# Decoder layer on one core: new homes for five tensors that hold ring places, x in quarters, last pair without a dispatch

## The chip, the cores and the metric

The kernel runs on one core of one Trainium2 chip (trn2), written in Bass with explicit semaphores: every engine (TensorE, VectorE, ScalarE, GpSimd, SyncE) has its own instruction stream, and SyncE and GpSimd also issue the transfers. The metric is the time of one execution on the device in microseconds (us).

## The reference

One layer over 256 tokens of width 1024, all in float32. The mixer normalises x, projects it with `w_in`, and runs three branches: causal differential attention (8 heads, two softmax maps each), a pooling mixer, and cross-attention into 256 memory tokens. Each branch has a gate; the merged result goes through `w_out` and is added to x. Then a mixture of 32 experts, 4 for each token:

```python
proj = rmsnorm(h, g_mix) @ w_in
q, k, v, u_pool, q_mem, gate_logits = split(proj)
g = sigmoid(gate_logits + b_gates)                 # three gates
h = h + (g[0]*y_attn + g[1]*y_pool + g[2]*y_mem) @ w_out
logits = rmsnorm(h, g_ffn) @ w_router + b_router   # top 4 of 32
g = minimum(xb @ w_gate[e] + b_gate[e], 7); u = clip(xb @ w_up[e] + b_up[e], -7, 7)
out = g * sigmoid(1.702 * g) * (u + 1) @ w_down[e] + b_down[e]
```

Each expert has three matrices of 1024 x 1024, 4.19 MB each: 402.65 MB in all, read once.

## The kernel before

**Mixer.** The weights come as 22 pieces (`PIECES`, L54) of two halves of 1 MB each, which SyncE loads in that order into five buffers `raw0` to `raw4`, in turn (`load`, L451; a half waits in `half_free`, L400, for the half five before it). A piece gives two units of 128 tokens (`UNITS`, L68). For the first piece TensorE multiplies in float32 (L1476). For all others ScalarE makes a rounded copy of the half (`hi`, L693), VectorE the remainder (`lo_whole`, L973), and TensorE three products for each block (L1483). The stationary operand is split in the same way: x into `XNT`, the memory into `MEMT`, the attention output into `OT`, the merged result into `MGT`. A unit writes one of three banks in turn and waits until the unit three before it has been read out of that bank (`bank_read`). Units 36 to 39 are branch a's gates (pieces ga0, ga1, halves 32 to 35), units 40 to 43 the attention map (wba0, wba1, halves 36 to 39), 44 to 47 `w_out`. `add_bias` (L1166) adds a gate's bias, which GpSimd has fetched into the gate's place (`gate_bias`, L615), and `gate_exp` (L704) applies the tanh. `merge` (L1185) multiplies with the branch. Head h of the attention takes the turn of the weights (`turn_a`), two units, the turn of the previous head's output and the values product. The order is written out by hand on every engine.

**Ring.** The experts' weights stream through a ring of ten places of 2 MB (half a matrix each, 20.97 MB). The ring lies over the mixer's buffers: the list `buffers` (L197) says which two share a place, so a half of the first fill can only be loaded once its two buffers are no longer used (`load_half(0, g)`, L488). Regions 0, 3, 4, 5 and 6 lie outside the ring.

**Expert stage.** 16 pairs of experts, 64 slots for each expert in a round (one round with these inputs). For a pair TensorE does: gate and up products of the first expert (L1773), the dispatch of the *next* pair's tokens (L1701), gate and up products of the second with the combination of the previous pair in between (L1761), and the down products of both (L1818). Half a matrix is 16 instructions. When a half has been used, SyncE issues the refill: for the first eight in quarters of the matrix (L550, L553), then halves, then whole matrices (L492); for the last pair halves again, and the very last half as two transfers of 1 MB (L515). The last combination (L1847) and four additions (L1392) end with four writes of the result (L574). VectorE and ScalarE run loops of two pairs in a loop over the rounds; TensorE and SyncE have the first round written out and jump over the code of further rounds.

## Time and profile before

| | us |
|---|---|
| median of 3 runs | 1213.95 (1213.93 to 1214.83) |
| the profiled execution | 1214.63 |
| its span, first to last instruction | 1212.8 |
| TensorE matmul busy | 1169.5 |
| VectorE, ScalarE, GpSimd busy | 436.5, 260.5, 43.7 |
| moved by DMA | 460.67 MB, mean 380 GB/s |

The profile cuts the span into 40 slices of 30.3 us and gives for each the busy share of each engine and the rate of the transfers. The granted TensorE clock has two levels, 1.2 and 2.4 GHz; its mean over the span is 0.990 of the upper one. A matmul's end is modelled, and busy TensorE is not TensorE at its peak. The chain of waits is followed back from the last instruction, at each step to what released it.

### The profile page before, as it was taken

Reading aid. Unit: us, or ns where it says so; the run is one execution under the profiler, and the core shown is the slowest. Engines: PE = TensorE matmul, PEld = TensorE weight load, DVE = VectorE, ACT = ScalarE, POOL = GpSimd, SP = SyncE. Lnnn points to the kernel's source line nnn. Section 1 sums busy time; section 2 is a strip of 40 time slices with the busy share of each in tenths; the row PEclk is TensorE's granted clock in tenths of the full one; section 3 lists DMA queues with packets and bytes.
Section 4 is the critical chain, followed back from the end, with each engine's and each line's share of the span. In section 5 each row is a group of like instructions: output and inputs, shape, how many; then the busy total and the mean of one; then the engine's idle time right before and its main releaser. Section 6 shows DMA issues by size and latency. Waiting matters only on the chain.

```text
span 1212.8 us, 13717 instructions
## 1 busy us (share of the span) xinstructions
PE 1169.5 (96%) x5436; PEld 581.0 (48%) x5436; DVE 436.5 (36%) x758; ACT 260.5 (21%) x463; POOL 43.7 (4%) x72
## 2 busy tenths in 40 slices
PE   9999999999999999999999999989898989899998
PEld 5888888888434344342434343433333343433342
DVE  5788798665222222222222121212122222221222
ACT  5655477542110110111010001101010101010101
POOL 1321101100000000000000000000000000000000
PEclk9999999999999999999999999999999999999999
DMA  9745645689999999999999999999999999999995
GB/s 384 267 148 185 214 142 186 224 363 394 406 427 431 427 432 432 431 432 431 430 431 430 429 429 432 431 432 431 431 431 432 432 432 431 431 431 431 425 428 232
DMA packets 28172, 460.67 MB, mean 380 GB/s; under 512 B 3216, under 2 KB 3984, under 8 KB 6608
## 3 DMA queue, kind: packets, MB, share of 16 engines
q1 hardware_dynamic: 27008, 456.34, 89.4%
q0 software_dynamic: 960, 3.41, 0.9%
q8 instruction: 49, 0.80, 0.3%
q14 instruction: 11, 0.09, 0.0%
q10 hardware_dynamic: 144, 0.03, 0.0%
HBM read 458.72 MB, written 1.05 MB: 379 GB/s over the span
## 4 chain that ended last, share of the span: by engine, by line
PE 66%; DMA 32%; issue 1%; DVE 1%; POOL 0%; SPq 0%; DVEq 0%; POOLq 0%
DMA experts_ring<-in_w_up 32%; PE bank L1773 25%; PE bank L1483 19%; PE bank L1818 7%; PE bank L1701 5%; PE bank L1761 2%; PE bank L1783 2%; PE bank L1447 1%; PE bank L1476 1%; PE bank L1784 1%; DMA raw<-in_mixer_halves 0%; PE bank L1847 0%; PE bank L1693 0%; PE bank L1602 0%; PE bank L1798 0%
## 5 line engine op out<-in xcount | busy, mean ns | idle before, releaser
L1773 PE MATMUL bank<-experts_ring,region 128*64 128x512 f32 x2048 | 468.4, 608 | 31.9 <-DMA experts_ring<-in_w_gate 21.2
L1773 PEld LDWEIGHTS bank<-experts_ring,region 128*64 128x64 f32 x2048 | 150.2, 139 | 325.5 <-issue 317.5
L1818 PE MATMUL bank<-experts_ring,region 128*64 128x512 f32 x1024 | 228.7, 596 | 2.1 <-DMA experts_ring<-in_w_down 1.9
L1483 PE MATMUL bank<-hi_split,region_split 128*128 128x512 f32 x400 | 151.3, 401 | 0.0
L1818 PEld LDWEIGHTS bank<-experts_ring,region 128*64 128x64 f32 x1024 | 73.6, 137 | 137.6 <-issue 136.4
L1483 PE MATMUL bank<-raw_split,region_split 128*128 128x512 f32 x336 | 130.9, 389 | 0.0
L944 ACT ACTIVATE region<-region 128x512 f32<-128x512 f32 x32 | 20.1, 629 | 452.3 <-DVE region L1409 452.3
L973 DVE TENSOR_TENSOR raw_split<-raw,hi_split 128x2048 fp32r<-128x2048 f32 x42 | 96.1, 2288 | 33.9 <-ACT hi_split L693 33.7
L1417 DVE TENSOR_SCALAR region<-bank 128x512 f32<-128x512 f32 x32 | 22.1, 692 | 236.7 <-PE bank L1784 236.7
L1409 DVE TENSOR_SCALAR region<-bank 128x512 f32<-128x512 f32 x32 | 22.1, 691 | 226.3 <-PE bank L1784 226.3
L1483 PEld LDWEIGHTS bank<-hi_split,region_split 128*128 128x128 f32 x400 | 75.1, 188 | 17.4 <-issue 2.6
L693 ACT ACTIVATE hi_split<-raw 128x2048 fp32r<-128x2048 f32 x42 | 80.1, 1912 | 14.7 <-DMA raw<-in_mixer_halves 14.7
L1432 DVE COPY region<-bank 64x512 f32<-64x512 f32 x32 | 22.2, 694 | 168.7 <-PE bank L1818 168.7
L1483 PE MATMUL bank<-hi_split,x_low_split 128*128 128x512 f32 x208 | 81.2, 390 | 0.0
L1483 PEld LDWEIGHTS bank<-raw_split,region_split 128*128 128x128 f32 x336 | 63.2, 188 | 12.4 <-issue 0.2
L1701 PEld LDWEIGHTS bank<-region 128*128 128x128 f32 x544 | 63.4, 192 | 2.0 <-DVE region L1333 0.5
L1701 PE MATMUL bank<-region 128*128 128x128 f32 x544 | 63.8, 275 | 0.4 <-DVE region L1333 0.4
L1761 PE MATMUL bank<-region 128*128 128x512 f32 x128 | 61.9, 606 | 0.0
L956 ACT ACTIVATE region<-bank 64x512 f32<-64x512 f32 x32 | 18.9, 590 | 152.3 <-PE bank L1818 152.3
L1392 DVE TENSOR_TENSOR region<-bank,region 128x512 f32<-128x512 f32 x68 | 43.9, 685 | 2.4 <-PE bank L1847 2.4
L1483 PEld LDWEIGHTS bank<-hi_split,x_low_split 128*128 128x128 f32 x208 | 39.0, 188 | 8.5
L1783 PEld LDWEIGHTS bank<-extra_split,region_split 128*128 128x128 f32 x64 | 11.9, 186 | 51.9 <-issue 51.9
(183 smaller groups left out, 760.2 us busy)
## 6 DMA issues: line engine op xcount, KB each, us to landing
experts_ring<-in_w_gate SPq DMA_DIRECT2D x26, 4096.0 KB, 36.6
experts_ring<-in_w_up SPq DMA_DIRECT2D x26, 4096.0 KB, 38.8
experts_ring<-in_w_down SPq DMA_DIRECT2D x26, 4096.0 KB, 39.2
raw<-in_mixer_halves SPq DMA_DIRECT2D x44, 1024.0 KB, 5.0
experts_ring<-in_w_up SPq DMA_DIRECT2D x10, 2048.0 KB, 11.1
experts_ring<-in_w_down SPq DMA_DIRECT2D x9, 2048.0 KB, 14.2
experts_ring<-in_w_gate SPq DMA_DIRECT2D x8, 2048.0 KB, 23.3
experts_ring<-in_w_gate SPq DMA_DIRECT2D x8, 1024.0 KB, 9.3
```

What stands on the lines that cost most here:

```text
L693: nc.scalar.activation(upper(H), raw(H), ACT.Copy).then_inc(hi_act, 1)
L973: nc.vector.tensor_tensor(lower(H), raw(H), upper(H), ALU.subtract).then_inc(lo_ready, 1)
L1392: nc.vector.tensor_tensor(X[:, t, h * HALF:(h + 1) * HALF], bank[banks[j]][:, :], X[:, t, h * HALF:(h + 1) * HALF], ALU.add).then_inc(y_ad ...
L1409: nc.vector.tensor_scalar(GS, bank[0][:, :], LIMIT, None, ALU.min).then_inc(g_read, 1)
L1417: nc.vector.tensor_scalar(US, bank[1][:, :], LIMIT, -LIMIT, ALU.min, ALU.max).then_inc(u_read, 1)
L1432: nc.vector.tensor_copy(OE[e * SLOTS:(e + 1) * SLOTS, HALF:D], bank[(2, 1)[e]][SLOTS:2 * SLOTS, :]).then_inc(o_hi, 1)
L1483: ins = nc.tensor.matmul(unit_bank(u)[:, :], a[:, k, toks], b[:, cols], start=(k == 0 and m == 0), stop=(k == k_n - 1 and m == 2))
L1701: ins = nc.tensor.matmul(bank[4 + half][:, b * P:(b + 1) * P], rows_[:, t, (4 * half + b) * P:(4 * half + b + 1) * P], PT[:, t, :], start= ...
L1761: nc.tensor.matmul(bank[6 + j % 2][:, :], PWT[:, t * P:(t + 1) * P], OE[:, h * HALF:(h + 1) * HALF], start=True, stop=True).then_inc(comb_ ...
L1773: ins = nc.tensor.matmul(dst[h * SLOTS:(h + 1) * SLOTS, :], XE[:, kk, e * SLOTS:(e + 1) * SLOTS], w[:, k, h * HALF:(h + 1) * HALF], start= ...
L1783: nc.tensor.matmul(dst[:, :], pick, BIAS_UP, start=False, stop=False)
L1818: ins = nc.tensor.matmul(bank[(2, 1)[e]][h * SLOTS:(h + 1) * SLOTS, :], AHT[e][:, k, half * SLOTS:(half + 1) * SLOTS], w[:, k, h * HALF:(h ...
```

## The change

Five tensors move, so that places of the ring come free sooner: regions 1 and 7 trade places in the ring; x transposed (`XNT[2]`) is loaded into region 9; the lower part of the attention output into region 3; the merged result `MG` into region 6 and its two split parts `MGT` into regions 4 and 6 (laid out by tokens first); branch a's gates into region 4, where V lives until the last values product; the normalised input of the router into region 5, the expert biases into the table's masks. Half 4 of the first fill goes out after the last query and key turn, half 9 after the last merge of branch m, halves 1 and 2 one mixer half sooner.

Transposed x comes in quarters and the first weight half in two parts; TensorE's four clearing products become two; the order of pieces is pool, q0, mk; the table, the memory rows and half 6 are loaded earlier, the band later. Branch a's biases are fetched after the last values product; `w_router` after the last wba unit, `b_down` after the last unit. A quarter of unit 15 goes ahead of a turn of memory probabilities, and the first half of unit 36 ahead of the last turn of weights.

The last pair makes no dispatch for a pair that doesn't exist. VectorE and ScalarE run the first round as five turns of three pairs and one pair alone, with further rounds under an If. The very last half comes as 1 MB and two of 0.5 MB, and the last combination and the writes go by column half first.

```diff
-PIECES = ["pool", "mk", "q0", "mv", "q1", ...
+PIECES = ["pool", "q0", "mk", "mv", "q1", ...
-        buffers = ("region9", "mem_low", "x_low", "region7", "hi4", ... "raw3", "region1", "region10",
+        buffers = ("region9", "mem_low", "x_low", "region1", "hi4", ... "raw3", "region7", "region10",
-        XNT = (rows_r(1), XLO_R, XLO)
+        XNT = (rows_r(1), XLO_R, rows(9, "k"))
-        G = {"p": rows(6, "t"), "m": rows(7, "t"), "a": rows(6, "t")}
-        MG = rows(8, "t")
+        G = {"p": rows(6, "t"), "m": rows(7, "t"), "a": rows(4, "t")}
+        MG = rows(6, "t")
-        OT = (rows_r(5), rows_r(2), None)
+        OT = (rows_r(5), rows_r(3), None)
-        MGT = (rows_r(10), rows_r(1), None)
+        MGT = tuple(region_r[i][:, :].rearrange("p (t k n) -> p t k n", t=NT, k=KD) for i in (4, 6))
-        HNT = rows(6, "k")
+        HNT = rows(5, "k")
...
             load_xT(0)
-            load(0)
+            sp.dma_start(raw(0)[:, 0:2 * HALF], half_source(0)[:, 0:2 * HALF]).then_inc(first_in, 16)
             load_xT(1)
+            sp.dma_start(raw(0)[:, 2 * HALF:4 * HALF], half_source(0)[:, 2 * HALF:4 * HALF]).then_inc(raw_in[0], 16)
+            load_xT(2)
+            load_xT(3)
             load(1)
...
-            for H in range(HALVES + 1, 2 * N0):
-                if H == 2 * PIECES.index("wba0") + 1:
+            for H in range(HALVES + 2, 2 * N0):
+                load(H)
+                if H == 2 * PIECES.index("ga1"):
+                    sp.wait_ge(qk_done, HEADS)
+                    load_half(0, 4)
+                if H == 2 * PIECES.index("wba0"):
+                    sp.wait_ge(merged, 4)
+                    load_half(0, 9)
                     sp.wait_ge(pv_done, HEADS)
                     biases()
-                    sp.wait_ge(merged, 4)
                     load_half(0, 0)
-                load(H)
-                if H == 2 * PIECES.index("wba1") + 1:
+                if H == 2 * PIECES.index("wba1"):
                     sp.wait_ge(oT_done, HEADS)
                     load_half(0, 1)
-                if H == 2 * PIECES.index("wo0") + 1:
+                if H == 2 * PIECES.index("wo0"):
                     sp.wait_ge(unit_done, UNIT_OF[("ga1", NT - 1, 0)] + 1)
                     load_half(0, 2)
             sp.wait_ge(unit_done, UNIT_OF[("wba1", NT - 1, 0)] + 1)
             load_half(0, 3)
-            sp.wait_ge(mgT_done, 4)
-            load_half(0, 4)
...
-            load_half(0, 9)
...
-            last = UNIT_OF[("wbp", 1, 1)]
-            pool.wait_ge(bank_read[last % 3], last // 3 + 1)
+            for h in range(3, HEADS - 1):
+                o_root(h)
+            pool.wait_ge(pv_done, HEADS)
             gate_bias(2, "a", 0)
+            o_root(HEADS - 1)
+            pool.wait_ge(unit_done, UNIT_OF[("wba1", NT - 1, 0)] + 1)
+            pool.dma_start(region[3][:, 1024:1280], w_router).then_inc(late_in, 16)
...
-            for _ in range(4):
+            for _ in range(2):
                 nc.tensor.matmul(bank[5][:, :], probT[:, 0, 0:P], probT[:, 0, :], start=True, stop=True)
...
             unit(14)
+            unit_k(15, 0, 2)
             mem_turn(0)
-            unit_k(15, 0, 4)
+            unit_k(15, 2, 4)
...
                 unit(21 + 2 * h)
+                if h == HEADS - 1:
+                    unit_k(22 + 2 * h, 0, 4)
                 turn_a(h)
...
-                for i in range(2):
-                    part = slice(i * 2048, (i + 1) * 2048)
+                for i, part in enumerate((slice(0, 2048), slice(2048, 3072), slice(3072, 4096))):
...
-                pe.wait_ge(hn_ready, NT)
-                dispatch(it + 1)
+                if more:
+                    pe.wait_ge(hn_ready, NT)
+                    dispatch(it + 1)
```

On VectorE the additions for units 36 and 37 stand together behind the remainder of half 36, ahead of the lower part of the last head's output and of the remainder of half 37.

## Rows read from the trace of the kernel before

**Rows 1.** The page: rate of the transfers in 40 slices of 30.3 us

```profile
GB/s 384 267 148 185 214 142 186 224 363 394 406 427 431 427 432 432 431 432 431 430 431 430 429 429 432 431 432 431 431 431 432 432 432 431 431 431 431 425 428 232
```

**Rows 2.** Windows, expert stage: us, each engine's busy time, clock, DMA share, GB/s

```profile
400.00:500.00 100.00, 100.00 (x472) 38.77 (x468) 22.48 (x43) 9.64 (x18) 0.00 (x0) 1.00 1.00 430
```

**Rows 3.** Chain of waits in order of time: start us, us, what

```profile
302.39 7.02 PE bank L1773 x32
...
355.74 6.87 PE bank L1773 x32
...
692.25 7.09 PE bank L1773 x32
...
750.52 7.09 PE bank L1773 x32
...
1122.37 39.15 DMA experts_ring<-in_w_up
1161.56 3.65 PE bank L1773 x16
1165.87 3.57 PE bank L1701 x32
```

**Rows 4.** Timeline of SyncE's transfers, 229 to 305 us: start, us, line

```profile
229.90 0.58 SPq L488 DMA_DIRECT2D experts_ring<-in_w_gate  x1
231.40 0.33 SPq L454 DMA_DIRECT2D raw<-in_mixer_halves  x1
...
294.73 0.80 SPq L488 DMA_DIRECT2D experts_ring<-in_w_down  x2
304.30 0.33 SPq L550 DMA_DIRECT2D experts_ring<-in_w_down  x1
```

**Rows 5.** Windows of 5 us where the stages meet, columns as in rows 2

```profile
225.00:230.00 5.00, 5.00 (x28) 4.22 (x27) 3.55 (x4) 1.34 (x5) 0.00 (x0) 1.00 0.03 11
...
305.00:310.00 5.00, 5.00 (x24) 1.54 (x20) 1.32 (x5) 1.76 (x2) 0.00 (x0) 1.00 0.92 333
```

**Rows 6.** Timeline of the first 8 us

```profile
1.32 5.12 PE L1492 MATMUL bank<-probT 128*128 128x512 f32 x8 [1.32 <-POOL probT L590]
...
4.84 1.23 DVE L988 TENSOR_TENSOR x_low<-x_low,small 128x1024 f32<-128x1024 f32 x1 [4.84 <-DMA small<-in_vectors]
...
7.16 14.00 PE L1476 MATMUL bank<-raw,x_low 128*128 128x512 f32 x32 [0.72 <-DMA raw<-in_mixer_halves]
```

**Rows 7.** Timelines near 240 us; landing of branch biases (L615), then b_down (L653)

```profile
224.47 0.69 DVE L1190 TENSOR_TENSOR region<-region,tmp 128x512 f32<-128x512 f32 x1
...
241.87 1.92 ACT L693 ACTIVATE hi_split<-raw 128x2048 fp32r<-128x2048 f32 x1 [5.76 <-DMA raw<-in_mixer_halves]
...
243.82 2.29 DVE L973 TENSOR_TENSOR raw_split<-raw,hi_split 128x2048 fp32r<-128x2048 f32 x1 [7.19 <-ACT hi_split L693]
...
245.06 0.39 PE L1483 MATMUL bank<-hi_split,region_split 128*128 128x512 f32 x1
...
DMA to landing us min/median/max: 3.9/4.6/5.9
...
DMA to landing us min/median/max: 7.0/7.0/7.0
```

**Rows 8.** Waits of TensorE up to 310 us, two of seven lines

```profile
PE bank L1615 <- issue: 0.7, 1, 0.7
...
PE bank L1447 <- DVE prob L1128: 0.6, 1, 0.6
```

**Rows 9.** Timeline of the end; landing of the last two transfers (L515)

```profile
1201.74 0.14 PEld L1818 LDWEIGHTS bank<-experts_ring,region 128*64 128x64 f32 x2 [0.35 <-DMA experts_ring<-in_w_down]
...
1204.03 0.69 DVE L1432 COPY region<-bank 64x512 f32<-64x512 f32 x1 [6.29 <-PE bank L1818]
...
1205.93 3.70 PE L1847 MATMUL bank<-region 128*128 128x512 f32 x8 [1.94 <-issue]
...
DMA to landing us min/median/max: 42.5/43.6/44.6
```

More of the change, by code:

```diff
@@ L660, in _ @@
             nc.gpsimd.memset(PWT, 0.0).then_inc(seed_clear, 1)
+            pool.wait_ge(unit_done, len(UNITS))
+            nc.gpsimd.memset(OE, 0.0).then_inc(seed_clear, 1)
+            pool.wait_ge(seed_clear, 2)
+            pool.dma_start(OE[0:EXPERTS, :], b_down).then_inc(late_in, 16)
         @block.scalar
@@ L744, in v_dst @@
                 return V[:, t, int(name[1]) * HALF:(int(name[1]) + 1) * HALF]
+            x_high(0)
+            x_high(1)
+            hi(2)
+            hi_after(0)
+            mem_high(0)
+            mem_high(1)
+            for t in range(NT):
+                act.wait_ge(x_in[t], 16)
+                square_of(t, X[:, t, :], t, JUNK)
+            hi_after(1)
+            evac(0, U[:, 0, :])
+            evac(1, U[:, 1, :])
+            hi_after(2)
+            square_evac(2, qk_dst(2))
+            hi_after(3)
+            square_evac(3, qk_dst(3))
+            act.wait_ge(mem_in, 16)
+            for t in range(NT):
+                square_of(2 + t, MEM[:, t, :], t, MEM[:, t, :])
             for u in (4, 5):
                 hi_after(u)
-                square_evac(u, qk_dst(u))
+                square_evac(u, KM[:, u - 4, :])
             for j in range(2):
@@ L960, in _, with round_copies @@
+            def round_copies(first):
+                with act.Fori(0, (PAIRS - 1) // 3) as d:
+                    for s in range(3):
+                        pair_copies(first + d * 3 + s, True)
+                pair_copies(first + (PAIRS - 1), False)
+            round_copies(0)
+            with act.If(n_rounds > 1):
+                with act.Fori(1, n_rounds) as r:
+                    xe_lower_half(r * PAIRS, r * PER_ROUND)
+                    round_copies(r * PAIRS)
         @block.vector
@@ L1010, in _ @@
             dve.wait_ge(gain_in, 16)
-            x_gained(0)
-            x_gained(1)
+            for i in range(4):
+                x_gained(i)
+            x_lower(0)
+            x_lower(1)
+            lo_whole(2)
+            lo_after(0)
             mem_gained(0)
@@ new lines, in round_results @@
+            def round_results(first):
+                with dve.Fori(0, (PAIRS - 1) // 3) as d:
+                    for s in range(3):
+                        pair_results(first + d * 3 + s, d * 3 + s, True)
+                pair_results(first + (PAIRS - 1), PAIRS - 1, False)
+            round_results(0)
+            with dve.If(n_rounds > 1):
+                with dve.Fori(1, n_rounds) as r:
+                    nc.vector.tensor_scalar(RANK, RANK, -float(SLOTS), None, ALU.add).then_inc(rank_ready, 1)
+                    dve.wait_ge(rank_ready, r)
+                    dve.wait_ge(slots_free, r * PAIRS)
+                    for t in range(NT):
+                        expert_slots(0, t)
+                    expert_weights(0)
+                    xe_upper_half(r * PAIRS)
+                    round_results(r * PAIRS)
```

351 lines of the change are left out of this document (163 added, 188 removed).

## The prediction, made before the changed kernel ran

> **What bounds the kernel now.** I read the share of each slice first, then the chain of waits in order of time, then windows of 5 us where the stages meet. The slices show two stages [rows 1]: up to about 225 us the DMA engines move 140 to 390 GB/s while TensorE is busy without a gap; from about 300 us they stay at 430 GB/s to the end. In the expert stage both engines look full [rows 2], so the chain has to decide. It starts the first expert product at 302.39, and the first pair takes 355.74 - 302.39 = 53.35 us, all TensorE. Much later a pair takes 750.52 - 692.25 = 58.27 us, and the chain runs through the landing of `w_up` [rows 3]. A pair reads six matrices of 4.19 MB, 25.17 MB, and that in 58.27 us is 432 GB/s, the rate of the windows. So the stage is bound by bytes. The first five pairs run at TensorE's pace only because the ring of ten halves (20.97 MB) was filled ahead.
>
> When does that stream of bytes end? It can't run ahead of TensorE by more than the ring. The last two halves of the first fill are issued at 294.73 and the next refill only at 304.30, when TensorE has read a quarter of its first half [rows 4]. Two halves are 4.19 MB, 9.7 us at 432 GB/s, so with about 2 us from issue to first bytes the ring is full at about 306.5. The share of the DMA engines dips just there, to 0.92 between 305 and 310 [rows 5]. The ring is full at the moment when TensorE begins to empty it. From then on the end is: TensorE's start, plus 2 us, plus the remaining (402.65 - 20.97) MB at 431 GB/s = 886 us, plus a tail. What the change can win ahead of 302.39 is therefore what it moves TensorE's own start, and hardly what it loads earlier.
>
> **Earlier loads of the ring.** With the new homes half 4 goes out after the last query and key turn, half 9 after the last merge of branch m, halves 1 and 2 some 8 us sooner. Before, halves 8 and 9 were together the last; after, half 8 alone is, issued at the same point of TensorE's work. It then lands some 5 us sooner, and the engines stand still until the first quarter is released at 304.30. Worth: what was left of the backlog at that point, 306.5 - 306.3, and the ragged end of two halves (0.08 of 5 us), 0.2 to 0.6 us. I take 0.4. The bounds are 0 and 3 us (all of the 2.5 us by which the refill's start could trail).
>
> **Start.** TensorE's four clearing products (eight instructions) end at 6.44; it then waits 0.72 us for the first half of weights and starts at 7.16 [rows 6]. The first transfers carry 0.52 + 1.05 = 1.57 MB until then. In the changed order the first products need 0.26 + 0.52 = 0.79 MB, 1.8 us less at 432 GB/s, so about 5.4. The gain multiply waits for the small vectors until 4.84 and is now 0.62 us for a quarter (half of 1.23), so 5.5. The eight clearing instructions take 5.12 us, 0.64 each, the 32 first real ones 14.00, 0.44 each, so some of the eight were slow. If all the slowness lies in the four that remain, these take 5.12 - 4 x 0.44 = 3.4 us and end at 4.7, still ahead of the data. TensorE starts at 5.55: 1.6 us gained. It keeps them if q0's pieces are split in time: x and the halves up to half 2 are 4.19 MB, which lands near 13; rounding and remainder take 1.92 + 2.29 us [rows 7], so 17.4, and unit 2 needs them at 19.5. Bounds 0 and 1.8: fewer products ahead and a pause behind them could leave the first real ones at the slow pace, at up to 0.4 us each. The granted clock is 1.00, the upper level, in every window I read there, which speaks against it.
>
> **Reordered mixer pieces.** q0 before mk, rotations earlier, the turns of the memory keys behind the second pool product: the same instructions on TensorE, nothing added. VectorE and ScalarE are busiest between 40 and 75 us, but TensorE had no gap there, and by an estimate from the durations in [rows 7] and 2.4 us for each megabyte each lower half is ready at least 1.5 us before its product (the tightest is the second half of mv: ready near 44.3, needed near 46.1). I take zero, with up to 1 us of loss as the far bound.
>
> **Two gaps that are now filled.** TensorE waits 0.6 us for the first memory probabilities and 0.7 us ahead of the turn of the last head's weights [rows 8]. The change puts a piece of the next unit (1.4 and 2.7 us of products) ahead of each. 1.3 us gained; 0 if their own operands are late, which nothing shows.
>
> **A new wait near 240 us.** Branch a's gates now live where V lived, so their 1 MB of biases can only be fetched when the last values product is done, 228.5, in place of 183. Half 9 goes out at 225.2, behind the merge that ends there [rows 7], into engines that stood idle before, 225 to 230 [rows 5]. Two things follow.
> First, unit 39 writes the bank of unit 36, which is released only by the addition of that bias; it starts one unit (24 products, 5.46 us) ahead of unit 40, which begins at 245.06 [rows 7], so at 239.6. Biases issued at 183 or before landed in 3.9 to 5.9 us [rows 7]; that would be 235 and cost nothing. But b_down, a tenth as large and issued while half 0 was under way, took 7.0 us. Served between the halves, the two bias transfers land at 235 to 240; the addition (0.75 us) then holds unit 39 by 0 to 1.2 us.
> Second, mixer half 37 is issued at 231.40 behind half 0 and lands at 241.87 (ScalarE waits 5.76 us for it); its lower part is ready at 246.1, and unit 40 needs it 12 products after 245.06, at 247.8. The slack is 1.7 us. Ahead of it there is now the rest of half 9 (about 0.6 MB at 230.3) and 1.05 MB of biases, less 0.13 MB of b_down, so 1.5 MB more, 3.6 us. Loss 1.9 us, into which the first falls. Bounds 0 and 8.3 (rival two). This is queued on VectorE ahead of the output's last lower part and the next additions, which have 2 us or more to spare.
> The Trainium skill ("DMA: Bandwidth & Descriptors", Queues, rings and completion order) says that an engine serves its queues in turn but drains a whole packet of one before it goes to the next. By it each bias transfer could wait for one half of 4.9 us, and both would land by 240 to 243: up to 4 us in place of 1.9. The 7.0 us of b_down agree.
> w_router moves behind the last wba unit, 268; VectorE needs it at 281, and even 7 us hide. b_down moves behind the last unit and is needed at 329.
>
> **The last pair.** Its dispatch is 3.57 us of TensorE [rows 3], which runs without a wait from 1161.56 on in the chain. But the last half is issued at 1156.7 to 1157.1 and lands 42.5 to 44.6 us later [rows 9], 1201.65, and TensorE waits for it 0.35 us at 1201.74. So the 3.57 us turn into a wait for bytes. What stays: behind the last landing there were two blocks of rows, 8 instructions, now one. Sixteen take 3.65 us, so four take 0.9. Bounds 0 and 1.5.
> The final products start at 1205.93 [rows 9], 1.2 us after VectorE's copy (1204.03 + 0.69) and about 2.5 us after the last product was issued; that is a jump over the code of further rounds, which stays. Starting them on the lower half first wins nothing, since the jump ends later than both copies; VectorE now has such a jump too, which would end 0.1 us behind the first final product: nothing.
>
> **Sum.** 0.4 + 1.6 + 0 + 1.3 - 1.9 + 0.9 = 2.3 us less. The profiled execution took 1214.63 with a span of 1212.8, against a median of 1213.95: the span becomes 1210.5, the median 1211.65, which I give as 1211.7.
>
> **Rivals.**
> One: the wait near 240 us does not come, since the queues interleave finely and half 9 is through by 230. Sum 4.2 us, 1209.75. For it: biases landed in 4.6 us before; against: half 37 had 1.7 us of slack only.
> Two (slower): the bias transfers are served only once SP's queue has drained. The place is unit 39, the price is landing minus 238.7. With halves 9, 0, 37, 38 and 1 queued, the landing could be near 247, and 8.3 us replace the 1.9: 1213.95 + 8.3 - 4.2 = 1218.0. It is slower than before from a landing at 243 on. For it speaks b_down's 7.0 us, against it that SP's queue is served in pieces.
> Three: the start doesn't come forward (small vectors, slow clock). 1.6 us gone: 1213.3.
> Four: bytes loaded earlier do count, since the stage is bound by bytes: 4.2 MB sooner are 9.7 us, 1204. Against: the ring is full at TensorE's start either way [rows 4, 5].
>
> **Chances.** Forecast 0.42 (its own range 1210.5 to 1213), rival one 0.20, two 0.20 (from 1215 to 1218), three 0.13, four 0.05. The range from 1209 to 1217.5 leaves out rival four and the far end of two. About 0.2% (2.4 us) is what a measurement of this kernel can tell from no change. Faster by more than that: rival one, rival four and a bit under half of the forecast, 0.44. Slower: two, 0.19. Within: 0.37.
>
> **What would show it.** After: TensorE's first real product near 5.6; its two gaps gone; new idle time of 1 to 3 us between 239 and 250, put down to the bias addition or the split of half 37; first expert product near 301.8; DMA share well under 0.9 in the 5 us before the first quarter is released; the last product ends about 1.4 us behind the last landing. I am wrong if the expert stage starts at the forecast time but the last landing is not 899 us behind it, or if a lower half is late between 40 and 75 us.

## The result and the profile after

The changed kernel takes 1225.57 us (median of 4 runs, 1223.39 to 1228.17) against 1214.39 for the kernel before: 1.0092 times its time, 95% interval 1.0071 to 1.0114. The forecast was 1211.7, its range ended at 1217.5. The profiled execution took 1226.12 with a span of 1224.3, 11.5 us more than before.

| | before | after | |
|---|---|---|---|
| first expert product starts [rows 3] | 302.32 | 308.42 | +6.1 |
| from there to the end of the last down product [rows 9] | 901.7 | 901.4 | -0.3 |
| from there to the end of the span | 8.8 | 14.5 | +5.7 |

The chain of waits in order of time (start us, us, what), around the two places where the time went:

```profile
227.75 0.60 POOL region L615
228.35 14.64 DMA region<-in_b_gates
243.02 0.76 DVE region L1182
243.82 23.82 PE bank L1510 x96
...
308.49 7.02 PE bank L1807 x32
...
1159.01 43.55 DMA experts_ring<-in_w_down
1202.69 7.10 PE bank L1853 x32
1209.82 0.60 ACT region L953
1210.42 4.30 issue
1214.72 6.45 PE bank L1883 x8
```

Branch a's biases are 1 MB in two transfers of 0.5 MB, one for each 128 tokens. The second takes 14.64 us from issue to landing and stands on the chain: in the kernel before the longest of the six such transfers took 5.9 [rows 7] and none was on it. At the end there are 4.30 us of "issue", where before there were 1.19, and eight final products that take 6.45 us in place of 3.70.

TensorE's waits up to 310 us (total, times, longest):

```profile
PE bank L1510 <- DVE region L1182: 5.2, 1, 5.2
PE bank L1510 <- DVE raw_split L982: 1.3, 2, 1.1
PE bank L1519 <- POOL probT L591: 1.3, 1, 1.3
PE bank L1503 <- DMA raw<-in_mixer_halves: 1.0, 1, 1.0
```

The two gaps of [rows 8] are gone. In their place stands one wait of 5.2 us (L1182 is `add_bias`) and one of 1.1 us for the remainder of a half. Of what the prediction named as signs, the ring did fill early: the share of the DMA engines is 0.58 from 305 to 310 us, against 0.92 before [rows 5]. Windows around the wait of 5.2 us (us, busy PE, PEld, DVE, ACT, POOL, granted clock, DMA share, GB/s):

```profile
240.00:241.00 1.00, 0.00 (x0) 0.00 (x0) 0.00 (x0) 0.00 (x0) 0.00 (x0) 0.93 0.91 377
241.00:247.00 6.00, 3.18 (x8) 2.51 (x9) 1.89 (x3) 3.12 (x4) 0.00 (x0) 0.50 1.01 425
247.00:248.00 1.00, 1.00 (x5) 0.83 (x4) 0.55 (x1) 0.41 (x1) 0.00 (x0) 0.66 1.17 500
```

TensorE stands still from 238.6 to 243.82. In that time its granted clock falls to 0.50, the lower level of 1.2 GHz, and is back at the upper level only at 248. The nine products behind the wait follow each other at 0.43 us in place of 0.23: another 1.8 us. TensorE came to this point 1.0 us ahead of the kernel before: 5.2 + 1.8 - 1.0 = 6.0, the whole delay of the expert stage.

The seven transfers that were under way together landed in this order: half 9 at 232.6, the first bias transfer at 236.2, the second at 243.0, half 0 at 243.1, mixer halves 37 and 38 at 245.5 and 248.0, half 1 at 252.9. So the biases neither waited for SyncE's queue to drain nor for whole halves. From 234 to 240 us the two queues moved about as many packets each (queue: packets, MB, share of the engines' time), but SyncE's (q1) are mostly of 16 KB and the biases' (q0, GpSimd's queue) of 4 KB:

```profile
q1 hardware_dynamic: 131, 1.99, 81.4%
q0 software_dynamic: 118, 0.44, 19.0%
```

That leaves the biases 0.44 MB in 6 us. One more thing was overlooked: unit 36, whose bank TensorE waits for, needs the first transfer only, which had landed 2.4 us before TensorE stopped. Its addition waits for both, because both count on one semaphore (`gbias_in`). No run gave each transfer its own. By an estimate half 37 would then have held TensorE: its remainder was ready at 249.7, and TensorE, 1.0 us ahead, would have needed it near 246.8, some 3 us earlier.

The end, in the timeline (idle time before, and its releaser, in brackets):

```profile
1209.82 0.59 ACT L953 ACTIVATE region<-bank 64x512 f32<-64x512 f32 x1 [7.05 <-PE bank L1853]
1209.82 0.69 DVE L1443 COPY region<-bank 64x512 f32<-64x512 f32 x1 [6.95 <-PE bank L1853]
1211.81 0.19 PEld L1883 LDWEIGHTS bank<-region 128*128 128x128 f32 x1 [2.91 <-issue]
1214.72 6.44 PE L1883 MATMUL bank<-region 128*128 128x512 f32 x8 [4.94 <-issue]
1214.72 0.29 PEld L1883 LDWEIGHTS bank<-region 128*128 128x128 f32 x1 [2.72 <-issue]
```

Both copies are done at 1210.5. The first load of weights comes at 1211.81, about where the kernel before began (1.9 us behind its last down product [rows 9]). Then nothing for 2.9 us, though by the code all waits stand ahead of both. In the kernel before the first loads and the first product stood together. After 4.94 us without a product TensorE runs the final ones at 0.8 us each.

So two theories were tested. First: the late biases are slow because the ring's halves share the engines with them, and that costs the 6 to 7 us ahead of the expert stage. Second: the pause at the end is the jump over the code of further rounds, dearer than before.

### The profile page after: what moved, and what is told of

It reads as the page before. It is cut to its first block, busy times and chain, and to the rows that moved or that the text cites. A ratio compares the mean times of both kernels' runs of the same rounds, so it can differ in the third digit from the quotient of the medians.

```text
span 1224.3 us, 13589 instructions
## 1 busy us (share of the span) xinstructions
PE 1167.5 (95%) x5400; PEld 577.1 (47%) x5400; DVE 434.8 (36%) x747; ACT 256.0 (21%) x456; POOL 49.6 (4%) x72
## 4 chain that ended last, share of the span: by engine, by line
PE 63%; DMA 34%; DVE 1%; issue 1%; ACT 1%; SPq 0%; POOL 0%; ACTq 0%
DMA experts_ring<-in_w_up 28%; PE bank L1807 25%; PE bank L1510 17%; PE bank L1853 7%; PE bank L1735 5%; DMA experts_ring<-in_w_down 4%; PE bank L1795 2%; PE bank L1817 1%; PE bank L1470 1%; DMA region<-in_b_gates 1%; DMA raw<-in_mixer_halves 1%; PE bank L1818 1%; DVE raw_split L982 1%; PE bank L1883 1%; ACT hi_split L690 0%
## 5 line engine op out<-in xcount | busy, mean ns | idle before, releaser
L1735 PEld LDWEIGHTS bank<-region 128*128 128x128 f32 x512 | 59.6, 192 | 1.9 <-DVE region L1349 0.5
L1735 PE MATMUL bank<-region 128*128 128x128 f32 x512 | 60.1, 275 | 0.4 <-DVE region L1349 0.4
```

The costliest lines, as they stand in the source:

```text
L1735: ins = nc.tensor.matmul(bank[4 + half][:, b * P:(b + 1) * P], rows_[:, t, (4 * half + b) * P:(4 * half + b + 1) * P], PT[:, t, :], start= ...
```

## The experiments

All ratios are to the kernel before, measured beside it, with 95% intervals; the changed kernel itself stands at 1.0092. Medians are of 4 to 11 executions; times inside a kernel (the last two columns, all in us) are of the one execution that was profiled.

| run | median us | ratio | first expert product | pause, final products |
|---|---|---|---|---|
| no bias for branch a | 1218.35 | 1.0028 (1.0017 to 1.0038) | 301.77 | 4.27, 5.29 |
| biases alone | 1226.41 | 1.0097 (1.0081 to 1.0114) | 309.1 | 4.34, 5.29 |
| ring late | 1220.34 | 1.0040 (1.0028 to 1.0052) | 303.07 | 4.60, 4.89 |
| region 8 only | 1218.43 | 1.0034 (1.0022 to 1.0046) | 301.23 | 4.54, 5.24 |
| straight end | 1220.25 | 1.0045 (1.0028 to 1.0062) | 307.40 | 0.72, 3.67 |
| straight end on VectorE alone | 1225.53 | 1.0090 (1.0075 to 1.0106) | 308.65 | 4.33, 5.27 |
| biases alone + straight end | 1222.64 | 1.0068 (1.0051 to 1.0085) | 309.1 | 0.73, 3.67 |
| region 8 + straight end | 1214.33 | 0.9998 (0.9989 to 1.0007) | 301.20 | 0.73, 3.67 |
| before + straight end | 1215.61 | 1.0005 (0.9996 to 1.0014) | 302.02 | 0.84, 3.67 |
| before + jump early | 1217.57 | 1.0026 (1.0016 to 1.0036) | 302.16 | 0.84, 3.67 |
| four clearing products | 1219.17 | 1.0046 (1.0030 to 1.0061) | 306.35 | 1.69, 3.69 |
| small clearing products | 1220.73 | 1.0055 (1.0039 to 1.0070) | 308.72 | 1.62, 3.69 |
| region 8 + jump early | 1213.24 | 0.9988 (0.9979 to 0.9997) | 300.90 | 0.74, 3.67 |
| the same + half in two | 1212.46 | 0.9985 (0.9976 to 0.9994) | 300.85 | 0.73, 3.67 |
| the same + fifth mixer half first | 1214.01 | 1.0001 (0.9992 to 1.0011) | 301.68 | 0.74, 3.67 |
| region 8 + half in two + small clearing products | 1214.64 | 0.9998 (0.9989 to 1.0007) | 301.53 | 2.55, 5.39 |

### The late biases

**No bias for branch a.** Its fetch and the wait for it are left out, and the addition is a multiplication alone.

```diff
-            pool.wait_ge(pv_done, HEADS)
-            gate_bias(2, "a", 0)
```

> Branch a's gates are written without their bias and its 1 MB is not fetched (left out: b_gates of branch a); all else is the changed kernel. Theory (two places: the late bias near 240 us, and the end): TensorE doesn't wait at 239, its clock stays at the upper level, the first expert product comes at about 301.4 in place of 308.5, the end stays as it is, 14.5 us behind the last down product: 1225.6 - 7.0 = 1218.5. Rival (half 37 behind the ring halves is late in any case): the stop moves to 247 and stays at 1 to 3 us: 1221 to 1223. Rival (the ring loads moved forward cost the expert stage itself): the start moves, the end doesn't: 1225.

1218.35, the first expert product at 301.77, no wait of TensorE over 0.4 us from 200 to 300 us: as the theory said. Half 37, which the forecast put first, is not late in this kernel.

**Biases alone.** SyncE issues half 37 first and lets nothing more go until the biases are there.

```diff
-                if H == 2 * PIECES.index("wba0"):
+                if H == 2 * PIECES.index("wba0") + 1:
+                    sp.wait_ge(gbias_in[2], 16 * NT)
                     sp.wait_ge(merged, 4)
                     load_half(0, 9)
```

> The biases of branch a are still fetched after the last values product, but SyncE issues mixer half 37 first and holds half 9, the expert biases and half 0 of the ring until they have landed. Theory (the transfer was slow only because it shared the engines with the ring): issue to landing falls from 14.6 to 4 to 6 us, no wait of TensorE at 239, first expert product at 301 to 302, 1218.5. Rival (it is slow by its own shape or place): landing again at 243, wait of 5 us, and the halves held back on top: 1226 to 1232. Rival (the ring's halves are now late for TensorE's start): start moves forward, yet the stream ends late: 1222 to 1225.

Two answers. The transfer is not slow by itself; issue to landing of all six bias transfers of the three branches (L616 here, shortest, median, longest):

```profile
DMA to landing us min/median/max: 3.8/4.7/6.1
```

6.1 us in place of 14.6. But the time didn't come back, 1226.41. What was held goes out at 234.2 to 237.4 in a bunch, and the mixer halves 38 and 39 are queued behind it:

```profile
256.94 0.67 PE L1511 MATMUL bank<-hi_split,region_split 128*128 128x512 f32 x1 [2.29 <-DVE region L1183]
263.67 0.60 PE L1511 MATMUL bank<-hi_split,region_split 128*128 128x512 f32 x1 [2.13 <-DVE raw_split L983]
```

```profile
251.98 1.92 ACT L691 ACTIVATE hi_split<-raw 128x2048 fp32r<-128x2048 f32 x1 [8.38 <-DMA raw<-in_mixer_halves]
```

ScalarE waits 8.38 us for a half, VectorE splits it and adds the next bias behind that, and TensorE stops twice, with the clock at 0.71 in the window around the first stop (255 to 260 us). I had expected 1218.5 and named a loss of this size only for a transfer that stays slow; the third possibility, that the mixer's own halves are now the late ones, I had missed. With the straight end on top the same two waits stand there:

> The previous two edits together. Theory (two causes that add): 1225.6 - 7.0 - 7.0 = 1211.6, that is 2.4 us less than the kernel before, which is the forecast's sum. Rival (the gains don't add, since an earlier TensorE meets a stream that ends no earlier): 1215 to 1218.

1222.64, where I expected 1211.6. Holding the ring back gained nothing: it cost 0.8 us on the changed kernel and 2.4 us on the straight end (1220.25 below). The straight end is worth 3.8 here.

**Ring late.** Halves 4 and 9 go back to where they were in the kernel before; the biases stay late.

```diff
-                    load_half(0, 4)
...
                     sp.wait_ge(merged, 4)
-                    load_half(0, 9)
```

> The changed kernel with halves 4 and 9 of the ring loaded late again, 4 behind half 3 and 9 behind half 8; the biases of branch a are still fetched after the last values product. Theory (the 14.6 us of that transfer are half 9's and half 0's packets on the other queue): without half 9 it lands in 6 to 9 us, by 237, TensorE doesn't wait at 239, first expert product at 301 to 302.5, 1218 to 1219.5; the ring 4 MB later filled costs nothing. Rival (half 0 and mixer half 37 are enough to hold it): landing 240 to 243, 1222 to 1225. Rival (an early ring is worth its bytes): the first pairs wait for bytes at 302 to 320 and the end comes 3 to 9 us later.

Landing of the six bias transfers (L615):

```profile
DMA to landing us min/median/max: 3.8/4.8/7.1
```

7.1 us: VectorE adds at 235.59, and TensorE doesn't wait at 239. So half 9, issued 2.8 us ahead of the biases, is what takes the transfer from 7.1 to 14.6 us (half 4, which also moved, had been issued at 206.6, over 20 us ahead of them). Half 37 is now the late one: its remainder starts at 246.02, and TensorE waits 1.5 us for it. That is the wait that the forecast had put at 1.9 us. The rate of the transfers is full from 300 to 310 (share 0.98 and 1.01), so the ring is still being filled there, later than in the kernel before [rows 5]; from the first expert product to the end of the last down product it is 902.5 us, against 901.4 of the changed kernel. 4.19 MB, 9.7 us of transfers, bought 1.1 us at most. The total, 1220.34, is above what I expected by that wait.

**Region 8 only.** The gates move to region 8, whose last use by others is over at 183, so that the biases can be fetched as early as before. Half 4 lies over it and waits for the last merge.

```diff
-        G = {"p": rows(6, "t"), "m": rows(7, "t"), "a": rows(4, "t")}
+        G = {"p": rows(6, "t"), "m": rows(7, "t"), "a": rows(8, "t")}
...
             load_half(0, 3)
+            sp.wait_ge(merged, 8)
+            load_half(0, 4)
```

> The changed kernel with one thing altered: branch a's gates in region 8 and their biases fetched at 183 (half 4 of the ring waits for the last merge for that); the end as changed, with its jump. Theory: first expert product at 301.2, pause at the end 4.3 to 4.9 us, 1218.3; so the late biases alone cost 7 us and the end alone 4 to 6. Rival (part of the loss at the end came from the late stage): more than 9 us less, 1215.

1218.43, first expert product at 301.23, final products behind 4.54 us of "issue". This kernel computes all of it, so the late biases cost 7 us (1225.57 - 1218.43); what is left above the kernel before is the end.

### The end

**Straight end.** The last combination and the last additions follow the first round directly, under `n_rounds < 2`; the further rounds have their own copy behind them.

```diff
+            with pe.If(n_rounds < 2):
+                last_combine(PAIRS)
             with pe.If(n_rounds > 1):
                 with pe.Fori(1, n_rounds) as r:
...
+                last_combine(n_rounds * PAIRS)
```

> The last combination and the last additions stand directly behind the code of the first round, under a condition on the number of rounds; TensorE and VectorE no longer jump over the code of further rounds ahead of them. Theory (TensorE's pause of 4.9 us at the end is the jump, and the slow clock follows from the pause): the final products start within 1 to 1.5 us of the copies, run at 0.46 us each in place of 0.81: 2.9 + 2.7 + some 1.5 us less, 1218.6. Rival (the pause is a semaphore or an operand that is late): nothing changes, 1225.6. Rival (the pause only moves, since the taken branch of the condition must fetch its code too): 1223 to 1225.

```profile
1209.35 3.67 PE L1878 MATMUL bank<-region 128*128 128x512 f32 x8 [0.72 <-issue]
```

The pause is 0.72 and the products are at full clock: the pause was the jump, and the slow products came of the pause. 5.3 us are back, not 7: from the end of the last addition to the end of the span it is now 4.65 us (1213.75 to 1218.4) against 2.4 before (1210.35 to 1212.8). The jump is still made, behind the final products, and the program isn't over until it is; the run with region 8 and the jump early, below, takes it away from there and has 2.5 us again.

**Straight end on VectorE alone**, TensorE's jump as it was:

> The changed kernel with the straight end on VectorE alone; TensorE still jumps over the code of further rounds. Theory (TensorE's own jump is the pause): still 4 to 5 us, 1224 to 1226. Rival (the jumps of three engines at the same moment delay each other's code): pause back to about 2 us and the products at full clock, 1220 to 1221.

1225.53, pause 4.33. It is TensorE's own jump; VectorE's was not what held it. ScalarE's jump, also new, was not tested by itself.

**Before + straight end** asks whether the kernel before pays too:

> The kernel before with its last combination directly behind the first round on TensorE (no jump ahead of it), nothing else changed. Theory (every jump over that code costs, before too): its pause of 1.94 us becomes 0.7, 1.2 us less, ratio 0.999. Rival (only the changed kernel's code is laid out badly): no change, ratio 1.000.

Pause 1.94 to 0.84, and the total unchanged (1.0005, where I expected 0.999): what the start of the products gains, the jump behind them takes. **Region 8 + straight end** has both edits:

> Branch a's gates go to region 8, so that their biases are fetched at 183 as in the kernel before; half 4 of the ring, which lies over region 8, waits for the last merge; half 9 still goes out early; the end is the straight one. Theory (late bias fetch and the jump are the two costs, ring halves loaded early are worth nothing): first expert product at 301 to 302, end 9 us behind the last down product: 1211.5 to 1213. Rival (half 9 out early delays mixer halves 37 and 38 as holding it back did in the run with the biases alone): a wait of 1 to 5 us between 240 and 265, 1214 to 1218. Rival (half 4 loaded late costs the stream): 1215.

1214.33, 0.9998, again above what I expected (1211.5 to 1213): the last down product ends at 1203.02, 1.0 us before that of the kernel before, the last addition 2.2 us before, and the span is 0.5 us shorter. Half 9 out early delayed nothing here.

**Four clearing products.** Why is the jump dearer than before, if the code behind it is the same? The shift of the code was tested by giving TensorE two of its clearing products back.

```diff
-            for _ in range(2):
+            for _ in range(4):
                 nc.tensor.matmul(bank[5][:, :], probT[:, 0, 0:P], probT[:, 0, :], start=True, stop=True)
```

> The changed kernel with four clearing products at the start again in place of two: eight more instructions (four loads of weights, four products) ahead of everything on TensorE, so that all of its later code lies that much further on in memory. Theory (the pause at the end is the fetch of the code behind the jump, and in the changed kernel the first products there lie in two blocks of code, so it is paid twice, 2.9 us each): with other positions the last products are fetched at once, the pause is about 2 us as in the kernel before, the products keep the full clock: 1225.6 - 5.7 = 1220. Rival (the pause has to do with what the other engines or the shorter last pair do): 4 to 5 us again, 1225. The start itself: first real product at 6.4 to 7, at most 0.9 later.

```profile
1209.51 0.30 PEld L1883 LDWEIGHTS bank<-region 128*128 128x128 f32 x2 [2.57 <-issue]
1209.52 3.69 PE L1883 MATMUL bank<-region 128*128 128x512 f32 x8 [1.69 <-issue]
```

Eight instructions at the other end of the program, and the pause is 1.69 us in one piece. The expert stage starts 2.1 us sooner as well: the biases landed at 241.1 in place of 243.0, and the wait was 3.5; why, stays open. The first real product started at 7.59, later than I had expected. **Small clearing products** (four of 256 columns) shift the code and leave the start alone:

> The changed kernel with its two clearing products of 512 columns written as four of 256: the same clearing time, and TensorE's later code eight instructions further on, as in the run with four clearing products. Theory (the pause at the end depends on where the code behind the jump lies): pause 1.7 us, final products 3.7 us, while the wait near 240 stays at 5 us: 1225.6 - 5.9 = 1219.7, first real product near 6.1. Rival (the longer pause had to do with the start being earlier, or with how long TensorE had idled near 240): pause 4 to 5 us, 1225.

The wait near 240 is 5.3 us as in the changed kernel, the pause 1.62. So it is position, worth 5.6 us of span (1218.7 against 1224.3). Two more runs ask for its period, with 64 and 32 tiny products more ahead of everything:

```diff
+            for _ in range(64):
+                nc.tensor.matmul(bank[5][:, 0:16], probT[:, 0, 0:P], probT[:, 0, 0:16], start=True, stop=True)
```

> The changed kernel with 64 tiny clearing products (16 columns) behind its two: each is four instructions of TensorE, so all later code lies 256 instructions further on. A shift of 8 took the pause at the end from 4.9 to 1.7 us. Theory (TensorE's code comes in blocks of a fixed size, and what counts is where the code behind the jump lies in its block; 256 is a multiple of the block): the pause is 4 to 5 us again, in two pieces with one load of weights between them, as in the changed kernel. Rival (a larger shift is as good as the small one, so it was something else that the small shift changed): 1.7 us. The Trainium skill (Advanced Engine Details and Errata, ISA Cache) gives the block as 256 instructions. The whole is later by the 64 products themselves, 10 to 25 us.

> The same with 32 tiny products, 128 instructions. Theory (the code behind the jump then lies in the middle of its block): pause 1.6 to 2 us in one piece, final products at 3.7 us. Rival (the block is 128 instructions or less): 4 to 5 us. The whole is later by the 32 products, 5 to 12 us.

Shifted by 256 instructions, then by 128:

```profile
1239.07 0.19 PEld L1885 LDWEIGHTS bank<-region 128*128 128x128 f32 x1 [2.42 <-issue]
1242.12 5.74 PE L1885 MATMUL bank<-region 128*128 128x512 f32 x8 [4.58 <-issue]
```

```profile
1224.02 3.70 PE L1885 MATMUL bank<-region 128*128 128x512 f32 x8 [0.76 <-ACT region L953]
```

With 256 the long pause is back, in the same two pieces with one load of weights between them. With 128 it is 0.76, less than the 1.6 to 2 that I expected, and TensorE waits for ScalarE's copy, not for its code. (Each is a single execution; the totals, 1252.9 and 1233.5, hold the tiny products, 27 and 14 us, more than I had allowed.)

The trace has a witness that I overlooked. It records the code's own transfers, in packets of 16.4 KB on a queue called `q8 instruction`: 49 in the kernel before and in the changed one, 50 with 256 or 128 more instructions on TensorE. In the changed kernel there is one packet between 1208.9 and 1210.2 us, ahead of the load of weights at 1211.81, and one between 1212.0 and 1214.5, ahead of the product at 1214.72:

```profile
q8 instruction: 1, 0.02, 4.4%
q8 instruction: 1, 0.02, 2.7%
```

| kernel | last down product ends | packet of code awaited starts | next load or product on TensorE |
|---|---|---|---|
| before | 1204.0 | 1202.8 | 1205.9 |
| changed | 1209.8 | 1209.1, 1212.2 | load 1211.8, product 1214.7 |
| small clearing products | 1209.9 | 1208.7 | 1211.5 |
| 256 further on | 1237.5 | 1236.3, 1239.5 | load 1239.1, product 1242.1 |
| 128 further on | 1223.3 | 1221.1 | 1224.0 |

From the start of a packet to the first instruction behind it it takes 2.5 to 3.2 us in these kernels (at 128 further on 3.0 at most, hidden behind the last products and the copy). So there are three cases: the code behind the jump is asked for early enough and is there (0.8), it is awaited once (1.6 to 1.9), or a second packet is awaited behind the first load (4.3 to 4.9, and the clock is lost on top). The kernel before and the one with small clearing products fetch a second packet too, 0.3 to 0.4 us behind their first final product, and don't wait for it; that the changed kernel needs it at once, because the edge of a block lies behind its first load, is what the shifts show. Why the first packet is asked for 0.7, 1.2 or 2.2 us ahead of the end of the down products stays open. The Trainium skill ("Advanced Engine Details and Errata", ISA Cache) says that an engine's instruction cache works in lines of 256 instructions; the runs agree with a block that divides 256 and not 128.

**Jump early.** If each jump over code that isn't there costs 3 to 5 us, it belongs where TensorE would wait anyway. The further rounds now come ahead of the last pair, first in the kernel before and on TensorE alone:

```diff
-            pair_products(0, 0, PAIRS - 1)
             with pe.If(n_rounds > 1):
+                pair_products(0, 0, PAIRS - 1)
                 with pe.Fori(1, n_rounds) as r:
...
+            with pe.If(n_rounds < 2):
+                pair_products(0, 0, PAIRS - 1)
+                last_combine(PAIRS)
```

> The kernel before with only this changed: on TensorE the code of further rounds lies ahead of the last pair. Theory: the pause of 1.94 us becomes 0.7 to 0.8 and nothing follows it: 1.2 us less, ratio 0.999; for comparison, the straight end, with the jump behind the final products, gave 1.0005. Rival: no change.

```profile
1149.99 3.15 issue
1153.15 7.09 PE bank L1773 x32
```

On the kernel before it loses 3 us: there the last pair has no slack, the 3.15 us push everything, and the last down product ends at 1206.6 in place of 1204.03. I had taken the waits of the middle of the stage for those of its end. With the last pair one dispatch (3.57 us) shorter the jump has room. The next run has it on TensorE, VectorE and ScalarE, with the gates in region 8:

> The kernel with branch a's gates in region 8, and on TensorE, VectorE and ScalarE the code of further rounds now lies ahead of the last pair, which has a copy of its own behind it: the jump is made while TensorE would wait for bytes, and nothing is jumped over at the end. Theory (with the straight end the jump only moved behind the final products, where it still ended last: 4.9 us from the last product to the end in place of 3.1): the final products start 0.7 us behind the last down product, the end comes 3.1 us behind them: 1.7 us less than the run with region 8, 1212.6, ratio 0.998 to the kernel before. Rival (the end is set by the four writes of the result, not by the jump): 1214.3 again.

1213.24, not quite the 1212.6 of the theory (in the profiled execution the products behind the jump also ran slow, 8.69 us for 32 in place of 7.09), and the end of the span is 2.5 us behind the last addition again. This is faster than the kernel before, by 0.12% (interval 0.03 to 0.21%).

**Half in two.** The second-last half of `w_down` as two transfers of 1 MB, each waited for by itself. First with an edit of the start (fifth mixer half ahead of the rows of x), then without it, then with the gates in region 8 and the shifted code:

```diff
+                for i in range(2):
+                    part = slice(i * 2048, (i + 1) * 2048)
+                    sp.dma_start(ring_half(PER_ROUND - 2)[:, part], rest[:, part]).then_inc(last_in[PER_PAIR + (-2, 2)[i]], 16)
```

> As the run with the jump ahead of the last pair, and two more edits: the fifth mixer half is loaded and converted ahead of the rows of x and their squares, and the second-last half of the experts' weights comes as two transfers of 1 MB, each waited for by itself. Theory (the last pair gained nothing because 32 products, 7.1 us, lie behind the landing of the second-last half, which comes whole): TensorE ends about 1.4 us behind the last landing, 0.9 to 1.2 us less; and the stall of 1.0 us at 32 goes, another 0.5 to 1.1: together 1.4 to 2.3 us less than the run with the jump alone. Rival for the first (the last landing moves back with the split): no gain at the end. Rival for the second (the fifth half lands no sooner than it is used, so bytes and not order decide): the stall stays.

> The run with the jump ahead of the last pair, and only the second-last half of the experts' weights in two transfers (the order of the start as changed). Theory (the split gives 1.2 us against the stream of bytes, but the last pair now begins behind a jump of 2.9 us and has 51.4 us of products, so TensorE itself is the bound): last down product 0 to 0.8 us sooner, 1212.6 to 1213.3; the order of the start was what made the other run's times spread. Rival (the split costs nothing and gives all): 1212.0.

> Gates of branch a in region 8, four small clearing products (TensorE's code moved on by eight instructions), the second-last half in two transfers, the jump at the end as in the changed kernel. Theory (each cause removed without moving the jump into the last pair): first expert product at 301.2, last down product at 901.3 minus 0.9 to 1.2 behind it, pause 1.7 us, products 3.7, end 3.1 behind them: 1211.8 to 1212.3, ratio 0.998. Rival (the split's own wait moves the code behind the jump into two blocks again): 1215 to 1216.

Whole, that half has 32 products (7.1 us) behind its landing; in the three kernels with region 8 it is 901.8 us from the first expert product to the end of the last down product. In two parts it is 900.6, 901.0 and 900.8, so 0.8 to 1.2 us less. TensorE's last 48 down products then run without a gap (10.52 us).

In total: 1214.01 (1.0001, 0.9992 to 1.0011), **1212.46 (0.9985, 0.9976 to 0.9994)** and 1214.64 (0.9998, 0.9989 to 1.0007). The second is the best kernel of this study, 0.7 to 2.9 us faster than the one before.

The first spread from 1211.6 to 1218.7, and its expert stage starts at 301.68, later than without the edit of the start, though its wait at 32 us is gone. That can't be put down to the edit: its first 32 real products took 16.1 us in place of 14.0, and in four other profiled executions that don't have the edit (no bias for branch a, region 8 only, straight end on VectorE alone, and the third run here) they took 15.5 to 16.3 and the wait at 32 us was gone as well. The granted clock reads 1.00 there in either case. What slows them, and what the edit is worth, stays open.

The third has its final products 2.55 us behind the last one and loses the clock (5.39 us for eight). My rival for it was code in two blocks again; but here a single packet of code, begun at 1202.0, comes before the first final product at 1204.9. It was asked for only 0.4 us ahead of the end of the down products (1202.3), where it is 1.2 us in most kernels; why, stays open.

## Why the prediction was wrong

- **Chain, bytes, ring.** Held. The end of the last down product follows the first expert product by 901.2 to 902.8 us in every kernel with whole halves and its jump at the end. Filling the ring 4 MB sooner was put at 0.4 (bounds 0 and 3), measured 0 to 1.1.
- **Start, 1.6 us.** Half right, then nothing. The first real product starts at 6.07, 1.1 us sooner, not 1.6: the data came later than I had from the bytes (TensorE waits 0.97 us for the half). Then this row undoes it:

```profile
32.15 0.47 PE L1510 MATMUL bank<-hi_split,region_split 128*128 128x512 f32 x1 [1.14 <-DVE raw_split L982]
```

- **Reordered mixer pieces, 0.** This is the step behind that row. ScalarE converts half 4 behind the squares of x, whose rows landed at 25.4. My estimate of "1.5 us ahead" looked from 40 to 75 us; the tight one was at 32. In the executions where the first real products are slow instead, TensorE is no further on behind them. Start and order together are worth about 0, inside the bounds given.
- **Two gaps, 1.3 us.** Held: both are gone, and region 8 only starts its expert stage 1.1 us before the kernel before.
- **The new wait near 240, -1.9 (bounds 0 and 8.3).** This step failed. It had the biases land at 235 to 240 and hold unit 39 by 0 to 1.2 us; the second transfer landed at 243.0, and TensorE stood for 5.2 us. Rival two named the right place and the right price, "landing minus 238.7": 4.3 us, 5.2 with the addition. But its mechanism, biases served only once SyncE's queue had drained, is not what happened: at 243.0 halves 0, 37, 38 and 1 were still to land. The biases were served in between, as the forecast had it, only with a fifth of the bytes. I chose the mild case by the row of b_down (7.0 us), which had one half under way ahead of it; here there were two, and 7.1 us with one against 14.6 with two is what the runs show. Nor did I see that the addition waits for the second transfer while it needs the first. The Trainium skill ("DMA: Bandwidth & Descriptors", Queues, rings and completion order) says that an engine takes a whole packet of one queue before it turns to the next. The trace agrees, 131 packets against 118 in 6 us. My estimate from it of 240 to 243, which took a packet for a whole half, met the landing by luck. The price also lacked the clock: 1.8 us of products at the lower level behind a stop that long. The loss was 7 us, inside the bounds and at their far end.
- **The last pair, 0.9.** Didn't come. The step "behind the last landing there are now four instructions" looked at the last landing alone. With that one early, the second-last is late: 7.1 us of products lie behind it. Splitting that half too brought 0.8 to 1.2 us.
- **"A jump over the code of further rounds, which stays", 0.** The worst step, and no rival covered it. I read 1.94 us from the row of before as the price of the jump. It is the price in one position of the code, and the change moved the code. The pause grew by 3.0 us, since a second packet of code is awaited behind the first load, and the clock that it cost is 2.7 more, in all 5.7.
- **Sum.** 2.3 forecast; the parts that hold come to about 1.3 (the two gaps). Against them 7 and 5.7: 1213.95 - 1.3 + 12.7 = 1225.4, measured 1225.6. Rival two, at 1218.0, was right in sign and in the place; it had neither the clock nor the end.

## What to carry to other kernels

A transfer whose home is free later than before has to be followed to its consumer with every larger transfer that is queued by then, on all queues, as the case to be beaten; and a ring that is full when its consumer starts gains almost nothing from being full sooner, while its loads stand in the way of the small one that is needed at once. A jump over much code has a price that an edit anywhere ahead of it can change: read the "issue" ahead of the first instruction behind it in both kernels, keep such jumps out of the tail, and put them only where the engine has that much slack in this very pair or stage, not on average.

## What was unexpected of the hardware

- A jump of TensorE over the code of further rounds left a pause of 0.8 (nothing to be seen), 1.6 to 1.9, or 4.3 to 4.9 us, by the position of the code alone; shifts of 8 and 128 instructions ended the long pause, a shift of 256 brought it back. In one more kernel it was 2.55. Code comes in packets of 16.4 KB that take about 1 us each, and the first instruction behind one that is awaited starts 2.2 to 3.2 us after the packet does.
- At the end and near 240 the products were at the lower clock behind stops of 2.55, 3.5, 4.3 to 4.9 and 5.2 us and not behind stops of 1.5 to 1.9 us; it cost 1.2 to 2.7 us for eight or nine products. With the biases alone it was at 0.71 around a stop of 2.3 us. In the last pair a stop of 2.92 us cost the clock (8.69 us for 32 products in place of 7.09) in one kernel and not in another, and stops of 3.15 and 3.35 us there did not, so the length of the stop alone doesn't decide.
- 1 MB of biases, in two transfers on GpSimd's queue, took up to 5.9 us with no half of the ring under way, 6.1 with one mixer half, 7.1 with half 0 and a mixer half behind it, 14.6 with half 9 ahead of it as well.
